# TensorE's last round of two expert pairs written directly behind the loop, with the further passes moved to the other branch

## What is computed

```
x (320, 1024); 32 experts, each token goes to its top 4
for expert e, on the tokens routed to it:
    h   = x_e @ w_gu[e] + b_gu[e]                 # 1024 -> 2048
    act = (clip(hu) + 1) * min(hg) * sigmoid(1.702 * hg)
    y_e = act @ w_down[e] + b_down[e]             # 1024 -> 1024
y = x + sum over experts of gate * y_e ; then RMSNorm
```

## Time and profile before

| | |
|---|---|
| median of 3 runs (lowest, highest) | 1419.26 us (1418.47, 1420.67) |
| profiled execution: its own time, its span | 1419.81 us, 1418.0 us |
| PE busy | 1346.4 us (95%) |
| DVE, ACT, POOL busy | 440.4, 260.4, 57.7 us |
| mean granted TensorE clock | 0.989 |
| read from memory | 465.33 MB |
| shares of the chain that ended last | PE 73%, DMA 19%, DVE 4%, issue 2% |

### The profile page before, as it was taken

One profiled execution on the slowest core, in us unless ns is written; L12 is line 12 of the kernel. 1 busy time (PEld: TensorE's weight loads), 2 busy tenths in 40 slices (PEclk: granted clock), 3 DMA queues, 4 the chain that ended last, 5 costly groups with the idle time before them and its releaser, 6 DMA issues.

```text
span 1418.0 us, 21208 instructions
## 1 busy us (share of the span) xinstructions
PE 1346.4 (95%) x8649; PEld 688.3 (49%) x8649; DVE 440.4 (31%) x880; ACT 260.4 (18%) x487; POOL 57.7 (4%) x111
## 2 busy tenths in 40 slices
PE   8989999999989999999999999889999898997997
PEld 5667789876656433433433434334343343332342
DVE  5998864451212313112211221112111131111112
ACT  4253512232231220110110201101011020010102
POOL 4361000000000000000000000000000000000000
PEclk9999999999999999999999999999999999998999
DMA  8961311038396699999999999999999999999992
GB/s 334 205 123 60 120 68 62 33 124 362 142 404 276 257 395 403 425 427 428 428 429 428 428 428 429 428 428 428 428 428 428 429 428 428 428 428 422 427 424 109
DMA packets 43336, 471.84 MB, mean 333 GB/s; under 512 B 4993, under 2 KB 10369, under 8 KB 11521
## 3 DMA queue, kind: packets, MB, share of 16 engines
q1 hardware_dynamic: 37264, 461.42, 78.3%
q10 hardware_dynamic: 6000, 9.41, 3.5%
HBM read 465.33 MB, written 5.48 MB: 332 GB/s over the span
## 4 chain that ended last, share of the span: by engine, by line
PE 73%; DMA 19%; DVE 4%; issue 2%; ACT 1%; SPq 0%; ACTq 0%; DVEq 0%
DMA big<-in_w_gu 18%; PE bank L1194 17%; PE bank L1243 15%; PE bank L685 10%; PE bank L1117 5%; PE bank L838 4%; PE bank L984 2%; PE bank L771 2%; PE bank L1307 2%; PE bank L1263 2%; PE bank L1124 1%; PE bank L1219 1%; PE bank L1292 1%; PE bank L849 1%; PE bank L1131 1%
## 5 line engine op out<-in xcount | busy, mean ns | idle before, releaser
L1194 PE MATMUL bank<-big 128*64 128x512 f32 x1920 | 426.9, 602 | 28.8 <-DMA big<-in_w_gu 28.7
L1194 PEld LDWEIGHTS bank<-big 128*64 128x64 f32 x1920 | 143.7, 138 | 309.0 <-issue 297.2
L1243 PE MATMUL bank<-big 128*64 128x512 f32 x960 | 209.4, 594 | 0.0
L685 PE MATMUL bank<-big 128*128 128x320 f32 (+1 forms) x688 | 187.0, 428 | 2.3 <-ACT big L1521 1.3
L685 PEld LDWEIGHTS bank<-big 128*128 128x128 f32 x688 | 129.0, 190 | 56.6 <-issue 6.0
L2242 DVE TENSOR_TENSOR big<-big,bank 128x320 f32<-128x320 f32 x120 | 58.6, 488 | 304.1 <-PE bank L1263 298.8
L2228 DVE TENSOR_SCALAR big<-bank 128x512 f32<-128x512 f32 x32 | 22.2, 693 | 396.6 <-PE bank L1194 366.4
L1243 PEld LDWEIGHTS bank<-big 128*64 128x64 f32 x960 | 70.0, 137 | 128.1 <-issue 126.4
L1590 ACT ACTIVATE big<-big 128x512 f32<-128x512 f32 x30 | 18.8, 627 | 454.0 <-DVE big L2228 454.0
L1358 ACT ACTIVATE big<-bank 128x320 f32<-128x320 f32 (+3 forms) x122 | 53.3, 437 | 196.2 <-PE bank L685 38.9
L1117 PE MATMUL bank<-big 128*128 128x512 f32 x192 | 85.4, 593 | 1.4 <-DVE big L2176 1.4
(11 more groups left out here) (398 smaller groups left out, 1089.1 us busy)
## 6 DMA issues: line engine op xcount, KB each, us to landing
big<-in_w_gu SPq DMA_DIRECT2D x128, 2048.0 KB, 25.1
big<-in_w_down SPq DMA_DIRECT2D x62, 2048.0 KB, 22.3
big<-in_dense SPq DMA_DIRECT2D x47, 1024.0 KB, 9.0
big<-u_windows ACTq DMA_DIRECT2D x32, 160.0 KB, 12.0
big<-in_w_down SPq DMA_DIRECT2D x4, 1024.0 KB, 15.2
big<-in_smw SPq DMA_DIRECT2D x1, 1408.0 KB, 19.6
big<-in_xT SPq DMA_DIRECT2D x2, 640.0 KB, 4.6
big<-in_consts SPq DMA_DIRECT2D x1, 1028.5 KB, 14.7
```

The costliest lines, as they stand in the source:

```text
L685: last = mm(b[:, 0:n], w[:, k, :], src[:, k, :], start=(k == 0), stop=(k == kt - 1))
L1194: last = mm(ps[n][part, :], xte[:, 2 * j + k, part], w[s][:, k, n * 512:n * 512 + 512], start=False, stop=end)
L1243: last = mm(ps[bank][part, :], actT[:, 4 * d + i, part], w[s][:, i, h * 512:h * 512 + 512], start=(d == 0 and i == 0), stop=end)
```

## The change

`all_passes` gets a parameter `in_line`, which TensorE alone sets. With it the branch behind the loop is turned round: where no expert has more than 64 tokens, the last round stands directly behind the loop, with round and pair numbers that are known when the program is built; otherwise the further passes run, and behind them a last round of their own with `final`. The further passes become a function. The program of the other engines stays as it was.

```diff
+        def further_passes(eng, most, two, next_pass=None):
+            with eng.Fori(1, PASSES) as p:
+                with eng.If(most > p * CAP):
+                    two(p * ROUNDS - 1, ROUNDS - 1)
+                    if next_pass:
+                        next_pass(p)
+                    with eng.Fori(0, ROUNDS - 1) as e:
+                        two(p * ROUNDS + e, e)
...
             with eng.Fori(1 if first else 0, ROUNDS - 1) as e:
                 two(e, e)
+            if in_line:
+                with eng.If(most < CAP + 1):
+                    two(ROUNDS - 1, ROUNDS - 1, last=True)
+                with eng.Else():
+                    further_passes(eng, most, two, next_pass)
+                    two(final, ROUNDS - 1, last=True)
+                return
             with eng.If(most > CAP):
-                with eng.Fori(1, PASSES) as p:
...
+                further_passes(eng, most, two, next_pass)
             two(final, ROUNDS - 1, last=True)
...
-            all_passes(pe, expert, last_pair, first=first_two)
+            all_passes(pe, expert, last_pair, first=first_two, in_line=True)
```

More of the change, by code:

```diff
@@ L427, in last_round, with all_passes @@
             return eng.value_load(most_i32[0:1, 1:2], min_val=0, max_val=(PASSES - 1) * ROUNDS) + (ROUNDS - 1)
-        def all_passes(eng, expert, last_pair, next_pass=None, first=None):
+        def further_passes(eng, most, two, next_pass=None):
[6 more added lines that the diff above has]
+                        two(p * ROUNDS + e, e)
+        def all_passes(eng, expert, last_pair, next_pass=None, first=None, in_line=False):
             def two(r, e, last=False):
@@ L440, in all_passes @@
                 two(e, e)
-            with eng.If(most > CAP):
-                with eng.Fori(1, PASSES) as p:
[L443 to L448, removed]
+            if in_line:
[5 more added lines that the diff above has]
+                return
+            with eng.If(most > CAP):
+                further_passes(eng, most, two, next_pass)
             two(final, ROUNDS - 1, last=True)
```

## The result

The changed kernel takes 1413.15 us (median of 6 runs, 1411.11 to 1415.49) against 1421.24 us of the kernel before beside it. The ratio is 0.9950 with a 95% interval of 0.9934 to 0.9966, that is 7.1 us less (4.8 to 9.4). The ratio isn't the quotient of the two medians, which differ by 8.1 us. Two later comparisons of the same kernel gave 0.9941 and 0.9945, 8.4 us (5.1 to 11.7) and 7.8 us (5.3 to 10.4). The forecast of 9.6 us had the sign and the mechanism right and was too large: it lies above all three measured values and outside the interval of the first, though the wider intervals of the other two hold it.

The account below looks back on a forecast made before the run. PE, busy 95%, was the bound, with a code-fetch hole behind the loop: 10.6 hole + 1.5 clock = 12.1, less 2.4 new wait, about 9.6 us gained; 1419.8 - 9.6 = 1410.2, median 0.5 lower: 1409.7 us, range 1408.4 to 1413.8.

Parts of the forecast that it names:

- What bounds the kernel now: PE busy 95%; behind the loop a 10.60 us hole from two sequencer stalls fetching code, 6.0 and 5.5 us.
- the stall belongs to leaving the loop: At the loop's exit: 6.0 us remain, only the second stall goes; gain 5.7 us, 1413.6 us, chance 0.10.
- The slower rival: In the last round: each 16 KB boundary stalls 5.5 us, 22 against 12.1 saved; 1429.2 us, chance 0.04.
- PE then meets the transfers again: At pair 14's last up step: PE waits 2.4 us for w_gu and starts the step at 1309.5.
- The gain is 9.6 us: At pair 15's start: it begins at 1342.5 where before it began at 1352.05, 9.6 us earlier.
- its own variant: At pair 14's last up step: 8.78 us in place of 7.09 behind the wait; 1411.4 us, 0.72 together with forecast.
- the clock's loss: Behind the hole, pair 14's bias and 128 up matmuls lose 0.95 + 0.56 = 1.5 us at reduced clock.
- It costs nothing: New far jump behind the last matmul: 6.0 us, ending 1.2 us ahead of SyncE; cost 0, bounds 0 and 4.3.

Follow-up runs that it names:

- the branch ahead of the loop: Kernel before with TensorE's branch on most > 64 moved ahead of the loop, each case with its own loop and last round: 1418.58 us, ratio 0.9983.
- the light loads: Pair 14's eight w_gu loads cut to their first halves: on the kernel before 1418.33 us, ratio 0.9978; on the changed kernel 1409.81 us, 0.9912.
- the moved target: Kernel before with 32 never-run bias matmuls added in the branch not entered, moving the far jump's target 128 instructions: 1413.95 us, ratio 0.9953.
- the end jump: Kernel before with a never-entered branch over two pairs' code behind TensorE's last matmul, so a far jump reaches the block's end: 1422.30 us, ratio 1.0010.

## Why the prediction held in its mechanism and missed in size

**What bounds the kernel now** held. The hole was two fetches of code, one in the branch and one at what the runs bear out as the next 16 KB boundary. That the second hangs on the target's place is shown by moving the target; the first is shown by the change itself: the same branch with its code behind it takes 78 ns. The rival that the stall belongs to leaving the loop is refuted by that row and by the branch ahead of the loop, which took 6.31 us. The slower rival is refuted too: the blocks of the last round come in on q8 without a hole. The queue after, from 1285 to 1402 us:

```profile
q8 instruction: 4, 0.07, 0.2%
```

These are four packets, and TensorE's timeline of that stretch shows no idle time put down to "issue".

**"PE then meets the transfers again"** held. The last up step came at 1309.89 against 1309.5 forecast, and lighter loads take the wait away. The wait was larger than forecast, 1.10 and 2.71 us in place of 2.4 in all, because pair 13's last up step was quick in this execution and pair 14 began at 1283.94 in place of 1285.2.

**"The gain is 9.6 us"** is the step that failed, by its size: the start of pair 15 came forward by 7.5 us. The step set a clean execution after against one before that wasn't clean. Pair 13's last up step in the profile before was slow, 8.78 us, and I wrote that in the loop the next wait absorbs this. Pair 13 has no next wait: behind the hole TensorE waits for no load, so its start of pair 15, 1352.05, has the 1.7 us in it. The profiles show this: the hole opens 34.7 us behind the start of pair 13's last up step in the kernel before, and 33.0 us with the light loads and with the moved target, where that step was quick. With a quick step (7.09 us) pair 15 would have begun at 1350.4. In four profiles with the hole at its old place (before, the end jump, the light loads, the moved target) pair 13's step was slow twice. Where the hole is gone, the slow step came in five of the six profiles with pair 14's wait; I had held it for a little less likely than not. Over all other waits of more than 2 us for w_gu, in the twelve profiles together, it came in 51 of 108, so the chance given wasn't far off, and five of six is too few to tell from it. Like set against like, the forecast's own numbers give 9.6 - 1.7 = 7.9 us at the start of pair 15. The profiled pair, slow against slow, is 7.9 less the 0.4 by which the last step started later than forecast, 7.5 as measured. One term errs the other way: the clock's loss in the 128 up matmuls behind the hole was taken as 0.56 us from 28.29, and the three other profiles with the hole at that place have 28.98, 29.09 and 29.86. Their mean with 28.29 would add some 0.8 us to the gain.

**"It costs nothing"**, with the bounds 0 and 4.3 on the jump at the end, asked only when TensorE arrives. This step failed as well, by the profiles. What it says of TensorE held: it comes in 5 us ahead of SyncE. Left out was that its two packets of 16 KB run among the stores of the output, for which SyncE does wait. In five profiles with the jump the stores of 128 KB land 3.2 to 3.6 us after their issue, and the way from the last matmul to SyncE's drain is 8.4 to 8.6 us; in seven without it these are 2.3 to 2.4 and 7.2 to 7.3. The 1.3 us are shown in the profiles, where adding the jump and taking it away both move them; that the packets hold up the stores is the reading that fits, and no run separates it from another effect of the jump. In the times they are not settled: adding the jump to the kernel before cost 1.4 us with an interval that holds zero, and taking it from the changed kernel gained nothing that the runs can tell.

With both steps put right, 9.6 becomes 7.9 in the start of pair 15 less 1.3 at the end, 6.6 us, or some 7.4 with the clock's loss as above; measured were 7.1, 8.4 and 7.8. The 18 runs of the changed kernel scatter by 2.0 us (standard deviation), so the last us stays open.

The absolute time has chance in it. The forecast of 1409.7 us started from 1419.26, the median of three runs; beside the changed kernel the one before took 1421.24. Of the 3.5 us between 1409.7 and 1413.15, 2.0 lie in that baseline and 1.5 in the gain. That 1413.15 lies within 1408.4 to 1413.8 is luck: it does only because that range was stretched for the rival of leaving the loop (1413.6), which the profile refutes; the forecast with its own variant ended at 1411.9.

## What to carry to other kernels

A jump over unused code costs its fetch where it stands, so put the common path in line; where that can't be, see where the target lies in its block, since a few unused instructions may spare the second fetch. A baseline taken from one profiled execution has that execution's accidents in it: before subtracting, ask of each slow piece whether a later wait absorbs it in the one kernel and in the other. And a fetch of code is traffic: at the end of a kernel ask what its packets stand in the way of, not only when the engine arrives.

## What the runs showed of the hardware

A far branch took 5.9 to 6.5 us in the six places where it began on transfers at full rate (6.01, 6.25, 6.31, 5.97, 5.91, 6.48; in the fourth, with the light loads, the share fell to 0.72 in the last 2 us). Behind the last matmul it took 3.3 to 3.7 us in five profiles (3.64, 3.30, 3.67, 3.72, 3.30), where the share of the transfers over the branch was 0.36 to 0.40. The stall right behind a jump fell alike, from 5.5 to 2.9 us, in the kernel before with light loads, where the share was 0.10. The price of a jump thus goes with the transfers under way; for the end of the kernel the place differs as well.

TensorE's loop over four packets of code turned five more times after its first turn without a fetch. The Trainium skill, Runtime: NRT & Kernel Launch, section Instruction fetch mechanics, states a window of two pages beyond which a taken branch must fetch; the far branches agree with that, and the back edges of this loop don't. In the same section it gives TensorE an instruction memory of 128 KiB, refilled in blocks of 16 KiB, and with that size both agree.

Waits of over 2 us for w_gu were followed by a step of 8.78 us in place of 7.09 in 56 of 114 cases in the twelve profiles. Behind pair 14's wait the granted clock was 0.60 from 1310.0 to 1313.4 in the changed kernel, and 1.00 from 1310.6 to 1314.0 in the one profile where the step was quick. Where light loads took that wait away, there was no slow step.
